# RWKV, LRU and PEER layer on one core: one weight split ahead of the key norms, squares at the end of the group before, m2 scores inside level 1, residual rows in eight loads, output banks taken by half, constants behind the first tile

## The reference, cut to what matters

```python
h = rms_norm(x, norm1_g)
proj = h @ w_in                                  # 2048 x (2048 LRU + 3360 RWKV columns)
y_lru = rg_lru_group(proj[..., :D_LRU], proj[..., D_LRU:2 * D_LRU], ...)   # conv, gates, scan, gelu
y_rwkv = rwkv7_group(proj[..., 2 * D_LRU:], ...)  # 16 heads of 64
x = x + jnp.concatenate([y_lru, y_rwkv], axis=-1) @ w_out
x = x + peer_ffn(rms_norm(x, norm2_g), peer_wq, peer_keys, peer_u, peer_v)
return rms_norm(x, normf_g)

# in rwkv7_group:
kk = (k * k_k).reshape(B, S, H, N)
kk = kk / jnp.maximum(jnp.sqrt(jnp.sum(kk * kk, axis=-1, keepdims=True)), 1e-12)   # the key norms
k = k * (1.0 + (a - 1.0) * k_a)
# step: state = state * w + (state @ -kk) * (kk * a) + v * k ;  y = state @ r
```

## Time and profile before

| | |
|---|---|
| median of three runs | 1966.7 us (1954.4, 1966.7, 1967.1) |
| the profiled execution | 1962.9 us, its span 1961.1 us |
| mean granted TensorE clock | 0.994 |
| busy: PE, DVE, ACT, POOL | 1906.1, 1561.5, 965.0, 525.1 us |
| DMA | 470 MB, 240 GB/s over the span |

### The profile page before, as it was taken

How to read it: one execution, slowest core, us unless ns; L and a number is a source line. 1 busy time by engine, 2 the same in 40 slices (tenths; PEclk the granted TensorE clock), 3 DMA queues, 4 the chain that set the end, 5 groups by cost and what they waited for, 6 DMA issues and landing times.

```text
span 1961.1 us, 34213 instructions
## 1 busy us (share of the span) xinstructions
PE 1906.1 (97%) x13424; PEld 1678.9 (86%) x13424; DVE 1561.5 (80%) x2398; ACT 965.0 (49%) x1387; POOL 525.1 (27%) x511
## 2 busy tenths in 40 slices
PE   8999999999999999999999999999999999999997
PEld 7887877777788888888888888888999999998886
DVE  6758575667544999997868878756988999999998
ACT  5535453565544444445444444445774544444444
POOL 0000000000000000000012222203777777877774
PEclk9999999999999999999999999999999999999999
DMA  7523333236655556555578888856989999999997
GB/s 242 194 84 123 90 117 98 66 116 213 205 186 171 186 191 193 187 190 193 188 223 285 282 276 282 282 190 212 320 267 351 395 386 390 383 387 386 387 396 276
DMA packets 151775, 470.32 MB, mean 240 GB/s; under 512 B 20192, under 2 KB 47872, under 8 KB 151104
## 3 DMA queue, kind: packets, MB, share of 16 engines
q1 hardware_dynamic: 118064, 331.23, 50.6%
q0 software_dynamic: 33552, 136.90, 18.7%
HBM read 438.63 MB, written 29.43 MB: 239 GB/s over the span
## 4 chain that ended last, share of the span: by engine, by line
PE 78%; DVE 11%; DMA 4%; issue 3%; ACT 3%; DVEq 0%; SPq 0%; ACTq 0%
PE ps L1782 78%; DVE sums L1109 3%; DMA vraw<-in_peer_v 2%; DVE lo L1101 2%; ACT hi L690 1%; DMA raw<-in_w_out 0%; DMA raw<-in_wq 0%; DMA got<-in_peer_v,row_ids 0%; DVE vlo L1642 0%; DVE a_lo L1698 0%; DVE zt L1199 0%; DVE xc L1109 0%; DVE hT L1109 0%; DMA oneJ<-oneJ_spill 0%; DVE TmTT L1334 0%
## 5 line engine op out<-in xcount | busy, mean ns | idle before, releaser
L1782 PE MATMUL ps<-hT,hi 128*128 128x512 f32 x2992 | 1065.7, 400 | 7.6 <-DVE lo L1101 7.6
L1782 PE MATMUL ps<-hT,lo 128*128 128x256 f32 x2992 | 839.3, 281 | 0.0
L1782 PEld LDWEIGHTS ps<-hT,hi 128*128 128x128 f32 x2992 | 563.0, 188 | 142.0 <-issue 9.2
L1101 DVE TENSOR_TENSOR lo<-raw,hi 128x1024 fp32r<-128x1024 f32 x406 | 492.0, 1223 | 197.7 <-ACT hi L690 192.9
L690 ACT ACTIVATE hi<-raw 128x1024 fp32r<-128x1024 f32 x406 | 423.5, 1060 | 420.6 <-DMA raw<-in_peer_u 370.8
L1782 PEld LDWEIGHTS ps<-hT,lo 128*128 128x128 f32 x2992 | 566.9, 189 | 0.1
L648 POOL DMA_INDIRECT got<-in_peer_v,row_ids x256 | 353.7, 1382 | 109.8 <-DVE sums L1109 73.0
L975 ACT ACTIVATE vhi<-vraw 128x896 fp32r<-128x896 f32 (+1 forms) x256 | 194.3, 766 | 250.7 <-DMA vraw<-in_peer_v 224.3
L1782 PE MATMUL ps<-vhi,a_hi 128*128 128x448 f32 x768 | 240.5, 368 | 6.9 <-DVE vlo L1642 4.9
L1109 DVE SCALAR_TENSOR_TENSOR sums<-got,wT,sums 128x704 f32<-128x704 f32 x256 | 243.8, 952 | 2.8 <-DMA got<-in_peer_v,row_ids 2.2
L1782 PE MATMUL ps<-vlo,a_hi 128*128 128x448 f32 x768 | 239.8, 367 | 0.0
(11 more groups left out here) (292 smaller groups left out, 1829.6 us busy)
## 6 DMA issues: line engine op xcount, KB each, us to landing
raw<-in_peer_u SPq DMA_DIRECT2D x256, 512.0 KB, 3.5
vraw<-in_peer_v SPq DMA_DIRECT2D x124, 448.0 KB
raw<-in_w_in SPq DMA_DIRECT2D x86, 512.0 KB, 3.5
vraw<-in_peer_v SPq DMA_DIRECT2D x124, 224.0 KB
raw<-in_w_out SPq DMA_DIRECT2D x32, 512.0 KB, 3.6
raw<-in_wq SPq DMA_DIRECT2D x32, 512.0 KB, 3.5
oneJ_spill<-madeJ POOLq DMA_DIRECT2D x64, 256.0 KB, 5.0
oneJ<-oneJ_spill SPq DMA_DIRECT2D x64, 256.0 KB, 4.9
```

What stands on the lines that cost most here:

```text
L1101: V.tensor_tensor(lo[n % NR][:, :], raw[n % NR][:, :], hi[n % NR][:, :].bitcast(F32), ALU.subtract).then_inc(lo_done, 1)
L1782: return nc.tensor.matmul(o, lhsT, rhs, start=start, stop=stop, skip_group_check=True)
```

## The change

Six edits.

1. The tile of `m(2)` is taken apart on ACT and DVE: `add_halves` and the first `hi` and `lo` piece stand ahead of the root of the key norms, the second `hi` and `lo` and the `result` behind it (on DVE behind rk). PE's order there stays.
2. From the second group on the squares of the keys are made at the end of the group before, ahead of ACT's wait for `y_f32`.
3. On PE the m2 scores stand between the two halves of `y` in level 1.
4. x2 comes in eight loads of 128 x 512, each behind a count of finished output pieces: 8, 10, to 22.
5. PE waits for the output banks t by t inside `rows_out`, not for all four ahead of the piece.
6. DVE's constants are made behind the first tile's `lo` pieces.

```diff
@@ POOL
             pool.wait_ge(sem("yR_lo"), GROUPS)
-            pool.dma_start(x2[:, :, :], a["x"].rearrange("o (t p) d -> p (o t) d", p=P)).then_inc(
-                sem("x2_in"), 16)
+            x_rows = a["x"].rearrange("o (t p) d -> p (o t) d", p=P)
+            for q in range(8):
+                t, part = q // 4, slice(512 * (q % 4), 512 * (q % 4) + 512)
+                pool.wait_ge(mm_done, 2 * T_OUT + 8 + 2 * q)
+                pool.dma_start(x2[:, t, part], x_rows[:, t, part]).then_inc(sem("x2_in"), 16)
@@ ACT
+            def key_squares(g):
+
+                for c in range(2):
+                    act.wait_ge(sem("shifted_done"), SHIFTED.index(ORDER.index(("k", 2 * g + c))) + 1)
+                    ins = nc.scalar.activation(sq[:, c], rkv[g % 2][:, 1, c], ACT.Square,
+                                               scale=col("k_k", 2 * g + c))
+                ins.then_inc(sem("sq_done"), 1)
...
-                for c in range(2):
-                    if g == 0:
-                        act.wait_ge(sem("shifted_done"), SHIFTED.index(ORDER.index(("k", c))) + 1)
-                    ins = nc.scalar.activation(sq[:, c], rkv[g % 2][:, 1, c], ACT.Square,
-                                               scale=col("k_k", 2 * g + c))
-                ins.then_inc(sem("sq_done"), 1)
+                if g == 0:
+                    key_squares(0)
                 m(0)
...
+                mid = marks.pop(0)
+                hi_piece(2 * mid + 2)
                 nc.scalar.activation(scal[:, 63:64], eps_c, ACT.Sqrt)
                 wait_full(act, "ss", g)
                 nc.scalar.activation(kn[:, :], bank("ss", g)[:, 0:8], ACT.Sqrt).then_inc(
                     freed("ss", g), 1)
-                m(2)
+                hi_piece(2 * mid + 3)
+                result(mid - 1)
                 m(3)
...
                 if g < GROUPS - 1:
+                    key_squares(g + 1)
                     act.wait_ge(sem("y_f32"), g + 1)
@@ DVE
-            for dst, name in ((hw0, "w0"), (ha0, "a0"), (hba, "ba"), (hbi, "bi")):
-                ts(dst, colr(name), 0.5, None, ALU.mult)
...
-            mark(ins, "identb_done", 1)
+            def constants():
+
+                for dst, name in ((hw0, "w0"), (ha0, "a0"), (hba, "ba"), (hbi, "bi")):
+                    ts(dst, colr(name), 0.5, None, ALU.mult)
...
+                mark(ins, "identb_done", 1)
...
                 tile(t)
+                if t == 0:
+                    constants()
...
+                mid = marks.pop(0)
+                add_halves(mid - 1)
+                lo_piece(2 * mid + 2)
                 wait_read(dve, "ss", g)
                 link(ts(kn[:, :], kn[:, :], 1e-12, 2.0, ALU.max, ALU.mult))
...
                 mark(ins, "rk_done", g + 1)
-                m(2)
+                lo_piece(2 * mid + 3)
+                result(mid - 1)
                 wait_full(dve, "kb", g)
...
-            dve.wait_ge(sem("x2_in"), 16)
+            dve.wait_ge(sem("x2_in"), 16 * 8)
@@ PE
-            def rows_out(n, act_hi, act_lo, banks, start, stop):
+            def rows_out(n, act_hi, act_lo, banks, start, stop, half=0):
 
                 for t in range(NT2):
+                    if start:
+                        for j in range(2):
+                            wait_free(pe, "out", 4 * t + 2 * half + j)
...
                     for half in range(2):
+                        if lv == 1 and half == 1:
+                            scores("m2", 2, lambda hp, c, tok: kt[hp, c, tok],
+                                   lambda hp, c, tok: ARt[hp, :, c, tok])
                         if lv == 1:
                             pe.wait_ge(sem("first_inverse"), 2 * g + half + 1)
...
-                    if lv == 1:
-                        scores("m2", 2, lambda hp, c, tok: kt[hp, c, tok], lambda hp, c, tok: ARt[hp, :, c, tok])
...
-                if c == 0:
-                    for t in range(NT2):
-                        for j in range(2):
-                            wait_free(pe, "out", 4 * t + 2 * half + j)
```

More of the change, by code:

```diff
@@ L1157, in _ @@
             turned_lo("x1", "g1")
-            for dst, name in ((hw0, "w0"), (ha0, "a0"), (hba, "ba"), (hbi, "bi")):
-                ts(dst, colr(name), 0.5, None, ALU.mult)
[L1161 to L1169, removed]
-            mark(ins, "identb_done", 1)
+            def constants():
+                for dst, name in ((hw0, "w0"), (ha0, "a0"), (hba, "ba"), (hbi, "bi")):
+                    ts(dst, colr(name), 0.5, None, ALU.mult)
+                ts(omu, colr("mu"), -1.0, 1.0, ALU.mult, ALU.add)
+                ts(hka, colr("k_a"), 0.5, None, ALU.mult)
+                link(ts(oka, colr("k_a"), -0.5, 1.0, ALU.mult, ALU.add))
+                V.tensor_copy(identb[:, :], ident[:, :])
+                for q in range(2):
+                    rows = slice(CHUNK * q, CHUNK * q + CHUNK)
+                    V.tensor_copy(idc[rows, :], ident[rows, rows])
+                    ins = V.tensor_copy(idcb[rows, :], ident[rows, rows])
+                mark(ins, "identb_done", 1)
             def result(t):
@@ L2140, in out_piece @@
                 rows_out(n, yh[:, c % CT], yl[:, c % CT],
-                         lambda t, j: bank("out", 4 * t + 2 * half + j), c == 0, c == N_OUT - 1)
+                         lambda t, j: bank("out", 4 * t + 2 * half + j), c == 0, c == N_OUT - 1, half)
             out_piece(*OUT_ORDER[0])
```

## The result

The changed kernel took 1949.9 us, the median of nine executions (1945.9 to 1959.0), against 1965.6 of nine of the kernel before: a ratio of 0.9934 [0.9919, 0.9948], about 13 us (the medians themselves lie 15.7 apart). A later series gave 1953.1 (six executions), a ratio of 0.9946 [0.9928, 0.9965]; all fifteen together have the median 1952.2. The forecast was 1954. Profiled span: 1948.1 us for 1961.1. One execution of all that follow, of a_best, took 2330 us at a mean granted clock of 0.75 and is left out.

A forecast was written before the change was run, and what follows sets the result against it. PE, busy 1906.1 of 1961.1 us, was taken as the bound, with DVE's chain leading in the groups. Gains 6.5 + 4.3 + 0.2 = 11.0 off 1962.9 or 1966.7 gave 1951.9 or 1955.7, hence 1954; range 1944 to 1963.

The forecast's parts named there:

- The constants: First tiles: PE's 1.26 us idle before piece 3 goes, but a later piece's unchanged landing leaves 0.2 of 1.4 us.
- rival A: First tiles: the piece behind g2 lands sooner and all 1.4 us stays, 1.2 more, giving 1952.8; chance 0.14.
- The split ahead of the norms: Groups' key norms: 1.74 us less DVE work behind `kn`, which comes 0.95 later; net 0.79, in group 0 only 0.27.
- The squares sooner: Key squares moved into ACT's wait for `yT`: 0 in group 0, 0.26 in group 1, 0.89 in groups 2 and 3.
- m2 inside level 1: Level 1: 32 score matmuls fill PE's idle time for the second `first_inverse`; 0.46 us a group, 1.84 in all.
- Banks and eight loads: Output stage: w_out's ninth `hi` no longer waits, PE's thirteenth piece 4.3 us sooner, the banks' 1.4 included.
- Clock: Half-clock stretches in groups 2 and 3: no change counted; bounds 1.7 us each, either way, for three.
- rival B: Group 3: steadier PE keeps its clock, 1.7 to 3.4 us more, about 1951; chance 0.10.
- Signs: Expected in profile: no gap before the tile after the norms, new waits before m0 and `kb`, one near 38 us.
- Rival C: Output stage: x's eight loads still delay w_out, only the banks' 1.4 remains, 2.9 us less, 1957; chance 0.10.
- rival E: Groups and output stage: the change does nothing, DVE and w_out being bound otherwise; 1963 to 1967; chance 0.04.
- D's mechanism: Groups: bunched PE waits at `bon` each drop the clock, 1.7 us a time; loses from seven extra stretches; chance 0.02.

The follow-up runs named there:

- a_best: Changed kernel with the second `lo` of the tile after the norms moved behind level 1's first `Ym` in groups 1 to 3 only; 1947.6 us, ratio 0.9911.
- b_m2: Kernel before with only the m2 scores moved between the halves of `y` in level 1; 1965.5 us.
- b_const: Kernel before with only DVE's constants moved behind the first tile's `lo` pieces; 1964.0 us in one execution.
- b_split_sq: Kernel before with only the split ahead of the key norms and the earlier key squares; 1955.7 us.
- b_x2: Kernel before with only x2 loaded in eight parts behind counts of finished output pieces; 1957.7 us.
- b_banks: Kernel before with only PE's wait for the output banks made t by t; 1953.3 us.
- a_again: Changed kernel run again with no edit; 1953.1 us, median of six, ratio 0.9946.
- a_idx: Changed kernel with PE waiting for its own three turns of `sel` before tile 65 of peer_u; 1957.5 us, median of eight, ratio 0.9964.

## Why the prediction was right

Of the sum, 6.5 + 4.3 + 0.2 = 11.0 us, the profiles show 7.3 + 4.7 + 1.4, 13.3 by piece 17 and 13.0 at the end. All parts have the forecast sign. The term of the constants was mis-sized through a wrong step, that of m2 through a row read too short.

- **The constants: 0.2 forecast, 1.4 measured.** The step that failed is "if it lands when it does now, PE stalls there". The landing at 36.7 was one execution's; five others without the edit have it by 35.3. I took the nearest row for a property of the schedule. The twelve operations bring 1.41 us in every profile. That the pair of profiles shows just 1.4 at `zw` is luck: 0.88 more came from the turns of x, ahead of the edit, and 0.95 was lost again to the slower pace of the tiles. That the gain stays is rival A's outcome, but not its reason: the load's landing moved by 0.5 to 0.8 us where its issue moved by 1.8, and it kept to the issue of g2's load. The Trainium skill (DMA: Bandwidth & Descriptors, "Queues, rings and completion order") has each DMA engine alternate between queues packet by packet; no run here shows whose turn it was, and a landing of 34.0 to 35.3, whichever of 26.0 or 28.3 the issue, doesn't support the jump ahead of g2 that I had drawn from it. The 1.2 us that I had put beside it was the right size for a wrong reason.
- **The split ahead of the norms: 0.27, 0.79, 0.79 and 0.79 forecast.** Alone it gave 0.84, 0.85, 0 and 0. Group 1 is right to 0.1. In group 0 I had let only the 0.27 us `bon` wait be PE's to win; 0.84 came by the end of level 1, so DVE leads there more than I had read. In groups 2 and 3 the clock took about 0.85 each in that one execution, as much as the split was to bring.
- **The squares sooner: 0, 0.26, 0.89, 0.89 forecast**, with the split 1.05, 1.68 and 1.68 for groups 1 to 3, 4.4 in all; the two together measured 1.22, 1.33 and 1.61, 4.2. That is 0.3 less in group 2 and nearly right in group 3. By difference the squares gave 0.37, 0.48 and 0.78: in group 2 about half of what I had read. Not foreseen: with the squares no wait for `bon` is over 1.5 us, and in this run and the changed kernel none has a half-clock stretch right behind it.
- **m2 inside level 1: 0.46 a group forecast, 0.64 measured in all four**, 2.6 for 1.84. The bound of 0.5 that I had set on it was wrong: this wait, counted from the last matmul's modelled end, is 0.2 us short of what PE wins in starts. The 1.8 that b_m2 shows from `zw` of group 0 to `yt` 3 is near the forecast by luck: group 1 gives 0.4 back at a place that I had not looked at, half-clock stretches took 0.4 in group 0 and 0.7 in group 3, and the missing one near 330 gave 0.6.
- **Groups together: 6.5 forecast, 7.3 measured**, with a stretch near 330 us in both profiles. By the end of level 1 the groups gain 1.41, 1.86, 1.99 and 2.30 us. The split with the squares, measured alone, and 0.65 of m2 add to 1.50, 1.87, 1.99 and 2.26: they hardly disturb each other.
- **Banks and eight loads: 4.3 forecast, 4.7 measured.** The chain that I wrote down step by step (ninth `hi`, table load, roots, `li`, `lo` 12) was followed up to `li`: counted from `yt` 3 the roots start 4.7 us sooner and `li` 4.2, for 4.7 and 4.25 in the working. The step that was mis-sized is the next: from `li` to the end of `lo` 12 I had taken all 12.8 us as dependent work, but 0.67 of it was DVE's wait for ACT's next `hi`, which fell to 0.22, and it now takes 12.34. So PE waits at the thirteenth piece for 0.20 us instead of about 1, then 0.56 at the seventeenth. That the banks' 1.4 lies within the total, not on top, is shown by the three runs (1.7, 4.6, 4.7).
- **Clock: nothing forecast.** The stretches of the earlier trace rows are now at 326 and 346, a third is gone:

```profile
325.50:329.00 3.50, 3.50 (x25) 3.00 (x22) 2.87 (x8) 0.59 (x2) 0.00 (x0) 0.54 0.00 0
345.50:349.00 3.50, 3.50 (x17) 3.12 (x18) 3.43 (x6) 2.97 (x3) 0.00 (x0) 0.61 0.01 5
```

The one near 330 is absent from b_m2, b_const, b_split_sq, b_x2 and most runs of the changed order, and there the way from level 1 of group 2 to `yt` 2 is 0.6 us shorter; so that was its price, not 1.7. It is no sign for rival B, as b_const and b_x2 have no edit in the groups. Rival B may have had a grain in it all the same: up to 560 us the clock is at half for 7 to 10 us in the four profiles without a group edit, for 3 to 7 in the seven of the changed order and its variants.

- **Signs.** No gap before the tile after the norms; 2.98 in front of `kb` in group 3; no `TmTT` or `yT` wait; the ninth `hi` behind the eighth: all there. The `bon` waits came, but two of the three (0.69, 1.40 and 1.24 us) are over the 0.5 to 1 that I had named. The wait at the thirteenth piece is 0.20, not about 1, and the wait near 38 us is not there, as said. Rival C is refuted by b_x2, rival E by the rows; D's mechanism may be what the split alone shows, on two stretches, far from its price of seven.

## What to carry to other kernels

A stall that a forecast puts back from one execution's landing should be checked against a second profile before it is used to cancel a gain: here it hid more than a microsecond. When work is taken out from behind a late step, look where the idle time gathers next; in its one execution the split alone gave 0.85 us where the new wait was under a microsecond and nothing where it was 1.8 or more and the granted clock fell behind it. Where a row says how long an engine waited, ask from which moment it counts. A bulk load that nobody needs yet, cut into parts tied to the consumer's progress, gave 4.6 us alone and 2.7 on top of the other edits. And a gain read from one pair of profiles should be followed back to the first row that differs: here 0.9 us of it stood ahead of every edit.

## What the runs showed of the hardware

PE has two paces at full granted clock. In a long stretch of equal pieces (eight pairs of matmuls of 512 and 256 columns) a piece takes either 2.773 or 2.830 us, for over a hundred pieces on end. Two windows of peer_u, the matmuls of PE counted in each (columns as above), in the kernel before, in b_banks and in the changed kernel's two profiles (after, then a_again):

```profile
650.00:950.00 300.00, 300.00 (x1732) 264.50 (x1731) 273.59 (x610) 144.48 (x166) 0.55 (x1) 1.00 0.59 190
1010.00:1310.00 300.00, 300.00 (x1700) 260.26 (x1699) 232.14 (x284) 140.37 (x160) 67.27 (x125) 1.00 0.83 269
```
```profile
650.00:950.00 300.00, 300.00 (x1732) 262.35 (x1732) 273.65 (x605) 144.08 (x164) 0.54 (x1) 1.00 0.58 190
1010.00:1310.00 300.00, 300.00 (x1733) 262.38 (x1732) 232.57 (x286) 143.33 (x164) 67.04 (x124) 1.00 0.83 272
```
```profile
650.00:950.00 300.00, 300.00 (x1733) 264.54 (x1732) 273.50 (x587) 144.23 (x165) 0.54 (x1) 1.00 0.60 190
1010.00:1310.00 300.00, 300.00 (x1701) 260.06 (x1700) 226.96 (x278) 140.53 (x161) 63.77 (x118) 1.00 0.83 265
```
```profile
650.00:950.00 300.00, 300.00 (x1699) 260.08 (x1698) 268.43 (x581) 142.01 (x162) 0.54 (x1) 1.00 0.58 187
1010.00:1310.00 300.00, 300.00 (x1733) 262.26 (x1732) 230.94 (x282) 143.48 (x164) 64.84 (x120) 1.00 0.82 270
```

1733 matmuls in 300 us or 1700, busy all the time and at clock 1.00: 2% apart. The same code has it one way in one execution and the other way in the next. In thirteen of fourteen profiles the kernel has each pace in one half of peer_u and changes at the small turns of `sel` between the halves; b_banks had the fast one in both, which made it 6.7 us faster there, and from the third piece to `zw` the first nine tiles differ by 0.95 us in the same way. A drain of PE ahead of the second half did not change it in the one profile of a_idx. What does is open; with differences of 1 us in question, profiles have to be compared between milestones that lie at the same pace.

An execution also places its half-clock stretches differently: 325 to 363 us in groups 2 and 3, in one or two runs each 150, 273, 278 or 515. One of them costs 0.6 (near 330) to 0.85 us (behind the waits for `bon`) where it could be read by difference between single profiles, less than the 1.7 that its window alone suggests.

A matmul of the short kind (64 columns, 0.22 us long in the timeline) does not hold up the next: in level 1 they start 0.03 us apart on average, and the wait whose row says 0.46 us is 0.67 us from the last start before it to the next.
